# A three-block decoder stack on one core: order of the gate and projection products, and the time at which some high parts of weights are made

## The reference, cut to what matters

```python
h = _rmsnorm(x, g_mix[l])
proj = h @ w_in[l]
q_a, k_a, v_a, cx, cb, cc, q_m, gate_logits = jnp.split(proj, IN_SPLITS, axis=-1)
...  # o_attn: dilated attention from q_a, k_a, v_a (width 256)
u = cc * cx
y_conv = wc[0] * up[:, :-2] + wc[1] * up[:, 1:-1] + wc[2] * up[:, 2:]
z_conv = cb * y_conv                                  # width 768
...  # o_mem: attention into the memory (width 512)
gates = jax.nn.sigmoid(gate_logits).reshape(b, s, N_BRANCH, d)
merged = (gates[:, :, 0] * (o_attn @ w_proj_attn[l])
          + gates[:, :, 1] * (z_conv @ w_proj_conv[l])
          + gates[:, :, 2] * (o_mem @ w_proj_mem[l]))
x = x + merged @ w_out[l]
...  # then a router and 32 experts, two of them per position
```

## Time and profile before

| | before |
|---|---|
| device time, median of 3 runs | 3719.6 us (3717.64 to 3726.79) |
| profiled execution | 3721.73 us, span 3719.5 us |
| mean granted clock of PE | 0.933 of full speed |
| busy: PE, PEld | 3326.3 us (89%), 2288.9 us (62%) |
| busy: DVE, ACT, POOL | 1128.7 us (30%), 1053.8 us (28%), 709.1 us (19%) |
| chain that ended last | PE 77%, DVE 8%, DMA 8%, ACT 3%, issue 3% |

### The profile page before, as it was taken

How to read it: one execution, slowest core, us unless ns; L and a number is a source line. 1 busy time by engine, 2 the same in 40 slices (tenths; PEclk the granted TensorE clock), 3 DMA queues, 4 the chain that set the end, 5 groups by cost and what they waited for, 6 DMA issues and landing times.

```text
span 3719.5 us, 38781 instructions
## 1 busy us (share of the span) xinstructions
PE 3326.3 (89%) x16196; PEld 2288.9 (62%) x16196; DVE 1128.7 (30%) x1781; ACT 1053.8 (28%) x1795; POOL 709.1 (19%) x344
## 2 busy tenths in 40 slices
PE   7998899987858999989889999988899988989996
PEld 5676678865537777756568876465686664333332
DVE  5333320223395555353231112375230121000001
ACT  3532342325432222123342331133321122111110
POOL 3022244432210000013134440000242221000001
PEclk9999999997879988789999999998999999999998
DMA  3231153321100000122122323210122238989996
GB/s 117 80 124 46 46 185 109 125 85 51 57 12 1 1 2 1 51 94 77 36 86 94 91 91 96 78 35 1 38 90 71 74 149 324 401 355 392 386 387 279
DMA packets 217628, 448.04 MB, mean 120 GB/s; under 512 B 14176, under 2 KB 191360, under 8 KB 204528
## 3 DMA queue, kind: packets, MB, share of 16 engines
q1 hardware_dynamic: 197664, 389.04, 28.7%
q10 hardware_dynamic: 9744, 36.18, 2.4%
q0 software_dynamic: 10048, 20.35, 1.6%
HBM read 502.14 MB, written 31.46 MB: 143 GB/s over the span
## 4 chain that ended last, share of the span: by engine, by line
PE 77%; DVE 8%; DMA 8%; ACT 3%; issue 3%; POOL 1%; SPq 0%; ACTq 0%; POOLq 0%; DVEq 0%
PE product_banks L563 13%; PE product_banks L564 12%; PE product_banks L565 12%; PE product_banks L535 8%; PE product_banks L1923 5%; DMA A<-in_w_down 4%; PE product_banks L1960 4%; DMA A<-in_w_up 3%; PE product_banks L627 3%; PE product_banks L1125 1%; PE score_banks L1106 1%; PE product_banks L1342 1%; PE product_banks L2396 1%; PE product_banks L586 1%; PE product_banks L587 1%
## 5 line engine op out<-in xcount | busy, mean ns | idle before, releaser
L472 POOL TENSOR_TENSOR Wr_parts<-Wr,Wr_parts 128x1024 fp32r<-128x1024 f32 x186 | 447.1, 2405 | 1431.9 <-ACT Wr_parts L449 1431.9
L564 PE MATMUL product_banks<-A_parts,Wr_parts 128*128 128x512 f32 x1408 | 560.0, 398 | 0.0
L449 ACT ACTIVATE Wr_parts<-Wr 128x1024 fp32r<-128x1024 f32 x186 | 196.0, 1058 | 729.8 <-PE product_banks L565 634.8
L1923 PE MATMUL product_banks<-A,Wr 128*64 128x512 f32 x1504 | 344.3, 600 | 12.9 <-DMA A<-in_w_up 11.8
L563 PE MATMUL product_banks<-H_parts,Wr_parts 128*128 128x512 f32 x728 | 298.6, 410 | 24.4 <-POOL Wr_parts L472 20.8
L564 PEld LDWEIGHTS product_banks<-A_parts,Wr_parts 128*128 128x128 f32 x1408 | 270.0, 192 | 61.7 <-issue 2.2
L563 PE MATMUL product_banks<-A_parts,Wr_parts 128*128 128x512 f32 x680 | 269.5, 396 | 31.8 <-DVE A_parts L485 15.6
L565 PE MATMUL product_banks<-H_parts,Wr_parts 128*128 128x512 f32 x728 | 292.3, 402 | 0.0
L472 POOL TENSOR_TENSOR shared_con_parts<-Wr,shared_con_parts 128x1024 fp32r<-128x1024 f32 x80 | 193.0, 2413 | 449.8 <-ACT shared_con_parts L449 449.8
L565 PE MATMUL product_banks<-A_parts,Wr_parts 128*128 128x512 f32 x680 | 267.2, 393 | 0.0
L1923 PEld LDWEIGHTS product_banks<-A,Wr 128*64 128x64 f32 x1504 | 117.2, 138 | 216.9 <-issue 213.5
(11 more groups left out here) (444 smaller groups left out, 5246.1 us busy)
## 6 DMA issues: line engine op xcount, KB each, us to landing
A<-in_w_gate SPq DMA_DIRECT2D x32, 2048.0 KB, 14.0
A<-in_w_up SPq DMA_DIRECT2D x32, 2048.0 KB, 17.8
A<-in_w_down SPq DMA_DIRECT2D x32, 2048.0 KB, 13.6
Wr<-in_m_w_up SPq DMA_DIRECT2D x32, 1024.0 KB, 5.4
Wr<-in_m_w_down SPq DMA_DIRECT2D x32, 1024.0 KB, 4.7
Wr<-in_w_in SPq DMA_DIRECT2D x32, 1024.0 KB, 5.4
Wr<-in_c_w_kv SPq DMA_DIRECT2D x16, 1024.0 KB, 5.0
expert_rows<-LB ACTq DMA_DIRECT2D x12, 1024.0 KB, 4.4
```

The costliest lines, as they stand in the source:

```text
L449: nc.scalar.activation(weight_parts(s)[0], loaded_part(s), ACT.Copy).then_inc(*mark("weights_high", s))
L472: nc.gpsimd.tensor_tensor(lo, loaded_part(s), hi, ALU.subtract).then_inc(*mark("weights_split", s))
L564: pe.matmul(bank[:, :], hi[:, k, :], x_lo, start=False, stop=False)
L1923: mm = pe.matmul(BK[r, 0 if kind == "gate" else 1, :], XT[b % 2][:, k * P + CAP * h:k * P + CAP * h + CAP], unit_rows((kind, b, h))[:, k, ...
```

## The change

In the plan, on PE and (through the plan) in SP's queue, the products `gate0`, `gate1`, `gate2` now stand one behind the other, and the products `proj0`, `proj1`, `proj2` behind them. The gate tiles of all three branches exist at the same time: they are written to tiles 34 to 41, 0 to 7 and 8 to 15. The last two groups held `cx`, `cc` and `cb`, so ACT's writing of them waits for the last tile of the convolution. ACT forms the high parts of the first two tiles of `cx` before its part of the dilated attention, and those of the first two tiles of `wout2` before the high part of the seventh merged tile. What is computed is the same.

```diff
+            for b in range(3):
+                lin(f"gate{b}", wi[:, 5120 + b * D:5120 + (b + 1) * D], D, split=True)
             for b, (w, k) in enumerate(((a.w_proj_attn_2, 256), (a.w_proj_conv_2, 768),
                                         (a.w_proj_mem_2, 512))):
-                lin(f"gate{b}", wi[:, 5120 + b * D:5120 + (b + 1) * D], D, split=True)
                 lin(f"proj{b}", w[0], D, k=k, w=256, evac="dve")
...
+        def gate_tile(b, j):
+            return tile((34, 0, 8)[b] + j)
...
             hnorm_act(act, 8, 20, take_va)
+            first_highs(act, "cx", 2)
             for i in range(NU + 1):
...
                     if b:
-                        act.wait_ge(*at("products_read_by_dve", (f"proj{b - 1}", j)))
-                    nc.scalar.activation(tile(34 + j), ps[:, :], ACT.Sigmoid).then_inc(
+                        act.wait_ge(*at("conv2_ready", 5))
+                    nc.scalar.activation(gate_tile(b, j), ps[:, :], ACT.Sigmoid).then_inc(
...
             for j in range(8):
+                if j == 6:
+                    first_highs(act, "wout2", 2)
                 high_part(act, ("merged", j), high(j), tile(42 + j), [("merged", j)])
...
             for b in range(3):
                 product(pe, f"gate{b}", hn_parts2, lambda k: [])
+            for b in range(3):
                 product(pe, f"proj{b}", branch[b], ready[b])
...
-                    nc.vector.tensor_tensor(dst, ps[:, :], tile(34 + j), ALU.mult).then_inc(
+                    nc.vector.tensor_tensor(dst, ps[:, :], gate_tile(b, j), ALU.mult).then_inc(
```

## The result

| | before | after |
|---|---|---|
| median | 3723.2 us (3717.6 to 3729.7, 4 runs) | 3684.0 us (3682.0 to 3687.5, 4 runs) |
| profiled execution: span | 3719.5 us | 3683.3 us |
| mean granted clock of PE | 0.933 | 0.935 |

The ratio is 0.9895 (95% interval 0.9875 to 0.9916): 39.2 us less between the medians. In two later comparisons the same kernel came to 0.9902 (0.9886 to 0.9918) and 0.9891 (0.9875 to 0.9907).

What follows compares the result with a forecast made beforehand. TensorE, busy 89% of the span, was taken to bound the kernel. Gains of 11.1, 13.1, 5.2 and 12.5 us, less 2.4 and 0.6, made 38.9 us and a forecast of 3681 us, range 3675 to 3691.

Steps and rivals of the forecast that it cites:

- early pair of `cx`: High parts of `cx` 0 and 1 formed ahead of the dilated loop: 11.1 us gained, 6.8 at the lower end.
- its cost at the rotary part: POOL's early low parts of `cx` hold up DVE in norms and rotary work: 2.4 us lost, bounds 0 and 4.7.
- gates ahead, with the new wait: Waits and slow matmuls go at `gate1` (13.1 us) and `gate2` (5.2); a new 0.6 us stall comes at `proj1`.
- early pair of `wout2`: High parts of `wout2` 0 and 1 before the seventh merged tile: 12.5 us gained, bounds 9.4 and 12.6.
- no reserve: At `wout2`, delayed low part 7 would be there at 3004.3 us; product 0 asks for it at 3004.3 or later.
- An expert stretch that is longer than before: Sign of being wrong: the distance from the end of `wout2` to the program's end was to stay.
- rival 3: The experts' weight stream does not start earlier, so the end stays at 3720 us; chance 0.03.
- Rivals 1 and 2: 1: small stalls and slow clock stay, 3693 us, chance 0.12; 2: only the early pairs work, 3698, chance 0.04.
- rival 4: Sustained dense gate products are clocked down to 1.2 GHz, making it slower, up to 3815 us; chance 0.03.

Runs made afterwards that it cites:

- filled: Kernel before, plus idle matmuls in TensorE's seven waits; 11.9 us less from the last dilated mix to the router's first product, whole-time ratio 0.9979.
- late_cx: Changed kernel, with ACT waiting for the last rotary operation before the early high parts of `cx`; ratio to before 0.9884, the second time 0.9881.
- order_only: Changed kernel without the early high parts of `cx` and `wout2`, so only the gates moved ahead of the projections; ratio to before 0.9951.

## Why the prediction was right, step by step

| step | predicted | in the trace after |
|---|---|---|
| early pair of `cx` | 11.1 | 25.04 (2648.37 to 2673.41) less 14.05 (2650.02 to 2664.07): 11.0 |
| its cost at the rotary part | -2.4 | -2.05 on DVE, -1.2 at the end of the dilated attention |
| gates ahead, with the new wait | 13.1 + 5.2 - 0.6 = 17.7 | 17.6; the wait is 0.79 |
| early pair of `wout2` | 12.5 | 12.8; start 1.53 us behind the last projection |
| sum | 38.9 | 40.2 (41.4 of the distance, less 1.2) |

The sizes came out because they were taken as distances between matmuls of the trace before, not as waits: 30.8 us of waits alone, of which 2.7 are left, would have given some 28 us, and filled shows that 11.9 of the 13.3 us beside them are the clock. That the time itself came so near is in part luck: 39.2 us between medians that scatter by 2 to 3, beside 40.2 in the trace. The 3684.0 us are 3 above the 3681 forecast, and the median of before had itself risen from 3719.6 to 3723.2 with a fourth run.

The step that was off, by 1.2 us, is the cost at the rotary part. That the second of POOL's low parts holds one DVE operation with two SBUF inputs, and the first none, came out as put (2.80 for 0.75 us). What I had not seen is that the first unit of the dilated attention runs at the lower clock in either kernel, and that the level rises within it. With the start 2.05 us later, more of it lay behind the rise: the mix of the first unit took 3.29 us instead of 4.21, 0.9 us back (before, then after).

```profile
2540.95 4.21 PE L1342 MATMUL product_banks<-A 128*64 128x128 f32 x20
2544.00:2546.00 2.00, 1.58 (x9) 1.23 (x9) 0.80 (x2) 0.00 (x0) 0.00 (x0) 0.82 0.00 0
```
```profile
2543.50 3.29 PE L1343 MATMUL product_banks<-A 128*64 128x128 f32 x20
2544.00:2546.00 2.00, 2.00 (x14) 2.00 (x13) 0.00 (x0) 2.00 (x4) 0.00 (x0) 0.66 0.00 0
```

A clock of 0.82 over these 2 us puts the rise from 0.5 to 1.0 near 2544.7 us before, 0.66 puts it near 2545.4 after. It comes 0.6 us later, 0.5 of which the whole program was late already, while the unit starts 2.5 us later. Why the rise did not move with the unit's work is not shown.

At `wout2` the prediction saw no reserve. There was one: beside POOL DVE's low part of the seventh merged tile lasted 2.89 us (row below), the eighth was done at 2976.1, and the first product asked for it at 2977.2.

```profile
2972.59 2.89 DVE L486 TENSOR_TENSOR A_parts<-A,A_parts 128x512 fp32r<-128x512 f32 x1
```

Of 40.2 us in the trace 36.2 are in the span. The stretch in front is 0.5 us later, and from the router's first product to the end the execution took 699.97 us instead of 696.39. An expert stretch that is longer than before was named as a sign of being wrong, and rival 3 (given back by the experts) would look like this. But late_cx, one kernel, took 700.7 us in one execution and 696.8 in the other, so 4 us is the scatter of that part; order_only, 17.2 us shorter in front of it, took 697.4. The three profiles of the kernel after lie at 698.7 to 700.0, and before has only one: a true loss of 1 or 2 us there can't be excluded. Rival 3, by which all of the gain would be lost, is out with the 39.2 us between the medians. Rivals 1 and 2 are out with the parts; rival 4 with the clock of 1.00 over 320 us of nearly unbroken matmuls.

## What to carry to other kernels

Where an engine waits between two equal pieces of work, measure from start to start and compare with an undisturbed piece: here 11.9 of 41.4 us were the lower clock behind the waits, which no table of waits shows. Work that is formed ahead runs beside something else; look up what that is, since a few us on an idle engine can hold the one that bounds (POOL beside DVE's operations with two SBUF inputs). And a prefetch chain of two slots can break at a change between kinds of work, as it did at `gate1` (5.66 us) and `wout2` (7.27 us). Forming the first pieces early mends it where their load has landed; where it hasn't, as at `gate1`, equal kinds have to stand together.

## What the runs showed of the hardware

A wait of 1.53 us (in front of `wout2`) left the clock at full level (the two products behind it took 11.0 us), as the gaps up to 1.50 us of the dilated attention do; behind each wait of 3.56 us and more the matmuls ran at the lower level for a time (0.76 on the mean of 2822 to 2840 us in the kernel before). A DVE reciprocal with one input was not touched by POOL's tensor-tensor (3.35 us in either kernel); the multiply with two SBUF inputs, begun beside POOL's second operation, which followed the first without a gap, ended 0.55 us behind it and so took 2.80 us instead of 0.75.
